# Value projection by halves of the contraction, the scaling of two attention heads on VectorE, and other PSUM banks at two places of the FFN

## What is computed

```python
D_MODEL, SEQ, DEPTH, D_FF = 1024, 256, 2, 2816       # D_A = D_B = 384, D_C = 256, B_HEADS = 6
...
def swiglu(x, w_gate, w_up, w_down):
    return (jax.nn.silu(x @ w_gate) * (x @ w_up)) @ w_down
...
def forgetting_attention(q, k, v, log_f):
...
        logits = logits + (c[:, :, q0:q1, None] - c[:, :, None, :q1])
...
        p = jax.nn.softmax(logits, axis=-1)
        outs.append(jnp.einsum('bhqk,bhkd->bhqd', p, vb))
...
def hybrid_mixer(x, w_in, ...):
    z = x @ w_in
    cuts = [int(v) for v in np.cumsum([D_A, D_A, D_B, D_B, D_B, B_HEADS])]
    a_x, a_gate, q, k, v, f_logit, c_u = jnp.split(z, cuts, axis=-1)
...
    o = jnp.concatenate([rms_norm(out_a, g_a), rms_norm(out_b, g_b), rms_norm(out_c, g_c)], axis=-1)
    return o.astype(x.dtype) @ w_out
...
    for l in range(DEPTH):
        x = layer_norm(ALPHA * x + 0.5 * swiglu(x, ffn1...), ln1_g[l], ln1_b[l])
        x = layer_norm(ALPHA * x + hybrid_mixer(x, ...), ln2_g[l], ln2_b[l])
        x = layer_norm(ALPHA * x + 0.5 * swiglu(x, ffn2...), ln3_g[l], ln3_b[l])
```

## Time and profile before

| | us |
|---|---|
| median of 3 runs | 1021.7 |
| lowest, highest | 1020.07, 1022.95 |
| the profiled execution | 1024.93 |
| its span on the core | 1023.1 |
| granted TensorE clock, mean | 0.989 |
| TensorE busy | 983.3 |
| VectorE busy | 700.4 |
| ScalarE busy | 538.8 |
| GpSimd busy | 332.3 |

### The profile page before, as it was taken

One profiled execution on the slowest core, in us unless ns is written; L12 is line 12 of the kernel. 1 busy time (PEld: TensorE's weight loads), 2 busy tenths in 40 slices (PEclk: granted clock), 3 DMA queues, 4 the chain that ended last, 5 costly groups with the idle time before them and its releaser, 6 DMA issues.

```text
span 1023.1 us, 14125 instructions
## 1 busy us (share of the span) xinstructions
PE 983.3 (96%) x5702; PEld 858.1 (84%) x5702; DVE 700.4 (68%) x820; ACT 538.8 (53%) x682; POOL 332.3 (32%) x398
## 2 busy tenths in 40 slices
PE   7899999999899999999999999999998989999997
PEld 6788888889887888888888888888988888888885
DVE  5676755788787756565788775657896876656556
ACT  4454545548883444444546444563788545444551
POOL 3029993042540600000053599900714342000000
PEclk9999999999999999999999999999999999999999
DMA  9755554474144665656476565545622356555541
GB/s 301 223 177 194 189 181 165 128 203 154 53 129 160 206 198 174 205 170 200 140 221 235 176 200 171 187 156 180 178 84 83 125 192 220 174 197 186 185 165 41
DMA packets 142383, 176.52 MB, mean 173 GB/s; under 512 B 11312, under 2 KB 126704, under 8 KB 142320
## 3 DMA queue, kind: packets, MB, share of 16 engines
q1 hardware_dynamic: 140592, 169.35, 51.8%
q0 software_dynamic: 1728, 6.29, 1.8%
HBM read 174.56 MB, written 1.05 MB: 172 GB/s over the span
## 4 chain that ended last, share of the span: by engine, by line
PE 82%; DVE 8%; ACT 3%; issue 2%; SPq 2%; POOL 2%; DMA 1%; DVEq 0%; POOLq 0%
PE bank L1691 28%; PE bank L1693 14%; PE bank L1662 11%; PE bank L1664 11%; PE bank L1663 11%; PE bank L1667 2%; SPq L430 2%; DVE wlo L1120 1%; ACT whi L714 1%; DMA raw<-in_ffn_w_up 1%; ACT u L922 1%; PE bank L1815 1%; POOL lngb L666 1%; PE bank L2005 1%; DVE xT_f L1377 1%
## 5 line engine op out<-in xcount | busy, mean ns | idle before, releaser
L1120 DVE TENSOR_TENSOR wlo<-raw,whi 128x2048 fp32r<-128x2048 f32 (+1 forms) x157 | 390.4, 2495 | 117.6 <-ACT whi L714 116.8
L1691 PE MATMUL bank<-xT,whi 128*128 128x512 f32 x1280 | 456.0, 400 | 6.2 <-DVE uT L1144 3.5
L1693 PE MATMUL bank<-xT,wlo 128*128 128x256 f32 x1280 | 360.0, 281 | 0.0
L714 ACT ACTIVATE whi<-raw 128x2048 fp32r<-128x2048 f32 (+1 forms) x157 | 297.2, 1897 | 14.8 <-DMA raw<-in_ffn_w_up 6.1
L1691 PEld LDWEIGHTS bank<-xT,whi 128*128 128x128 f32 x1280 | 241.2, 188 | 67.2 <-DVE uT L1144 4.9
L1693 PEld LDWEIGHTS bank<-xT,wlo 128*128 128x128 f32 x1280 | 242.5, 189 | 1.2
L1662 PE MATMUL bank<-whi,act_hi 128*128 128x512 f32 x376 | 148.7, 395 | 0.0
L1664 PE MATMUL bank<-whi,act_lo 128*128 128x512 f32 x376 | 146.9, 391 | 0.0
L1663 PE MATMUL bank<-wlo,act_hi 128*128 128x512 f32 x376 | 146.7, 390 | 0.0
L545 POOL TENSOR_TENSOR xtok<-xn,lngb 128x1024 f32<-128x1024 f32 x10 | 30.2, 3018 | 332.2 <-DVE xT L1409 332.2
L762 ACT ACTIVATE gs<-bank 128x512 f32<-128x512 f32 x40 | 23.9, 598 | 170.4 <-PE bank L1693 170.4
(11 more groups left out here) (318 smaller groups left out, 1337.7 us busy)
## 6 DMA issues: line engine op xcount, KB each, us to landing
raw<-in_ffn_w_up SPq DMA_DIRECT2D x44, 1024.0 KB, 5.4
raw<-in_ffn_w_down SPq DMA_DIRECT2D x44, 1024.0 KB, 4.9
raw<-in_ffn_w_gate SPq DMA_DIRECT2D x43, 1024.0 KB, 5.3
raw<-in_w_in SPq DMA_DIRECT2D x12, 1024.0 KB, 5.3
raw<-in_w_out SPq DMA_DIRECT2D x8, 1024.0 KB, 5.1
raw<-in_w_in SPq DMA_DIRECT2D x12, 512.0 KB, 5.1
lngb<-in_ln_g POOLq DMA_DIRECT2D x6, 512.0 KB, 4.1
lngb<-in_ln_b POOLq DMA_DIRECT2D x6, 512.0 KB, 5.5
```

Source lines behind the costliest of these rows:

```text
L714: A.activation(piece(whi, n, 8, PC)[:, :, cols], piece(raw, n, 8, PC)[:, :, cols], ACT.Copy).then_inc(hi_done, 1)
L1120: V.tensor_tensor(piece(wlo, n, 8, PC)[:, :, cols], piece(raw, n, 8, PC)[:, :, cols], piece(whi, n, 8, PC)[:, :, cols].bitcast(F32), ALU.s ...
L1691: T.matmul(bank[bnk + ft][:, :], hi[:, k, c], xT[:, k, :, :].rearrange("p a n -> p (a n)"), start=k == 0, stop=False)
L1693: ins = T.matmul(bank[bnk + ft][:, 0:SEQ], lo[:, k, c], xT_hi[:, k, :], start=False, stop=k == KD - 1)
```

## The change

1. **Value projection.** Pieces 0 and 1 of the mixer now hold the same 390 columns for contraction tiles 0 to 3 and 4 to 7. Events 0 and 2 sum in one bank (0), events 1 and 3 in another (1). There are 48 matmuls of 390 columns in a layer and not 48 of 256 and 48 of 134. Both splits have 1560 columns and not 2048 and 1072, and each load 1560 columns. The copies out are two for each token tile; the semaphore `f_evac` is gone, and the counts in `z_free` follow.
2. **Scaling.** Heads 0 and 1 are scaled on VectorE, between its reciprocals and the splits of pieces 8 and 9 (`ahead_mix(6)` and `ahead_mix(7)`). Heads 2 to 5 stay on GpSimd.
3. **FFN entry.** The up rows of token tile 1 go to bank 6 and not 5. TensorE waits for the Silu of tile 0 ahead of them, and no longer for the product ahead of the second half of `gate(f, 1)`.
4. **Parameters.** The wait for `par_ready` moves from ahead of `gate(f, 2)` to between its halves.

```diff
@@ -78,11 +78,11 @@
 QCOL = 2 * DA
-ZPIECES = [4 * DA, 4 * DA + PC, NIN - DC, 0, PC, None, None, None, 2 * PC]
+VCOL, VW = 4 * DA, DB + HEADS
+ZPIECES = [None, None, NIN - DC, 0, PC, None, None, None, 2 * PC]
...
-VT_W = DB - PC + HEADS
...
+        def body(t, n):
+            width = 4 * VW if n % LAYER_N in (MIX_BASE, MIX_BASE + 1) else 8 * PC
+            return t[:, slot(n), 0:width]
...
-        TOK_BANKS = ((6, 7), (4, 5))
+        TOK_BANKS = ((6, 7), (4, 6))
 
         def z_bank(e):
-            return (0, 2, 1, 3)[e] if e < 4 else 5 if e < 6 else e % 2
+            return e % 2 if e < 4 else 5 if e < 6 else e % 2
...
@@ block.sync @@
                 for m, col in enumerate(ZPIECES):
-                    if col is None:
+                    if m < 2:
+                        load(mix + m, win[L, :, 4 * m:4 * m + 4, VCOL:VCOL + VW], 4, VW)
+                    elif col is None:
...
@@ block.gpsimd @@
                 pool.wait_ge(ys_gelu, 16 * L + 16)
-                attn_scale(0)
-                attn_scale(1)
                 pool.wait_ge(oc_done, 2 * L + 2)
...
@@ block.scalar @@
-                A.activation(piece(whi, n, 8, PC)[:, :, cols], piece(raw, n, 8, PC)[:, :, cols], ACT.Copy).then_inc(hi_done, 1)
+                A.activation(body(whi, n), body(raw, n), ACT.Copy).then_inc(hi_done, 1)
...
-                    if f == 0:
-                        split_hi(base + FFN_N + 1, slice(0, VT_W))
-                    else:
-                        ahead(base + LAYER_N + 1)
+                    ahead(base + FFN_BASE[f] + FFN_N + 1)
...
                 def values_out(t):
-                    z_wait(t)
-                    A.activation(vv[:, t, 0:PC], bank[2 * t][:, 0:PC], ACT.Copy).then_inc(ly.z_evac, 1)
                     z_wait(2 + t)
-                    A.activation(flog[:, t, :], bank[2 * t + 1][:, DB - PC:VT_W], ACT.Copy).then_inc(f_evac, 1)
-                    A.activation(vv[:, t, PC:], bank[2 * t + 1][:, 0:DB - PC], ACT.Copy).then_inc(ly.z_evac, 1)
+                    A.activation(flog[:, t, :], bank[z_bank(t)][:, DB:VW], ACT.Copy).then_inc(ly.z_evac, 1)
+                    A.activation(vv[:, t, :], bank[z_bank(t)][:, 0:DB], ACT.Copy).then_inc(ly.z_evac, 1)
...
@@ block.vector @@
-                V.tensor_tensor(piece(wlo, n, 8, PC)[:, :, cols], piece(raw, n, 8, PC)[:, :, cols],
-                                piece(whi, n, 8, PC)[:, :, cols].bitcast(F32), ALU.subtract).then_inc(lo_done, 1)
+                V.tensor_tensor(body(wlo, n), body(raw, n), body(whi, n).bitcast(F32), ALU.subtract).then_inc(lo_done, 1)
...
                     if n == 0:
-                        split_lo(base + FFN_N + 1, slice(0, VT_W))
+                        split_lo(base + FFN_N + 1)
...
-                    vec.wait_ge(f_evac, 2 * L + 2)
+                    vec.wait_ge(ly.z_evac, 3)
...
+                def attn_scale(h):
+                    vec.wait_ge(ly.rrec_done, h + 1)
+                    V.tensor_scalar(prob[h % 2][:, 0:P], prob[h % 2][:, 0:P], rrec[:, h, 0:1], None, ALU.mult)\
+                        .then_inc(ly.pn_done, 1)
+                    V.tensor_scalar(prob[h % 2][:, P:], prob[h % 2][:, P:], rrec[:, h, 1:2], None, ALU.mult)\
+                        .then_inc(ly.pn_done, 1)
...
                 blocks_out()
                 attn_recip(0)
+                attn_scale(0)
                 attn_recip(1)
+                attn_scale(1)
                 ahead_mix(6)
...
@@ block.tensor, first_pair @@
+                    pe.wait_ge(ly.silu_done, f * (PAIRS + 1) + 1)
                     rows(u, 1, TOK_BANKS[1][1]).then_inc(pieces_used, 1)
...
@@ block.tensor, gate @@
                     if q == 1:
                         pe.wait_ge(ly.silu_done, silu_count(f, 0))
-                        features(base + gate_pos(f, q), 4, (ly.hid_done, silu_count(f, 0)))
+                        features(base + gate_pos(f, q), 4)
                     else:
                         pe.wait_ge(parts_added, gate_sums_done(L, f, q - 1))
-                        features(base + gate_pos(f, q), 4)
+                        features(base + gate_pos(f, q), 4, (par_ready, L + 1) if f == 0 and q == 2 else None)
...
                     down(f, 0)
-                    if f == 0:
-                        pe.wait_ge(par_ready, L + 1)
                     gate(f, 2)
...
@@ block.tensor, z_free and z_event @@
-                        pe.wait_ge(ly.z_evac, {6: 1, 7: 2}.get(e, e - 3))
+                        pe.wait_ge(ly.z_evac, {6: 2, 7: 4}.get(e, e - 3))
...
+                    c = slice(h * P, (h + 1) * P)
+                    if e in V_EVENTS:
+                        hi, lo = piece(whi, n0, 4, VW), piece(wlo, n0, 4, VW)
+                        k0 = 4 * (e // 2)
+                        for k in part:
+                            ins = mm3(bank[z_bank(e)][:, 0:VW], xT_hi[:, k0 + k, c], xT_lo[:, k0 + k, c], hi[:, k, :],
+                                      lo[:, k, :], k0 + k == 0, k0 + k == KD - 1)
+                        if part[-1] == 3:
+                            ins.then_inc(ly.z_half if h == 0 else pieces_used, 1)
+                        return
...
-                z_event(0)
-                z_event(2, range(0, KD // 2))
+                z_event(0, range(4))
+                z_event(2, range(0, 2))
                 turn_rows(ly, 0, 1)
-                z_event(2, range(KD // 2, KD))
+                z_event(2, range(2, 4))
                 pe.wait_ge(ly.xT_lo_done, 4)
-                z_event(1)
-                z_event(3)
+                z_event(1, range(4))
+                z_event(3, range(4))
```

More of the change, by code:

```diff
@@ L299, in trunk @@
         q_ones = sem("q_ones")
-        f_evac = sem("f_evac")
         oc_done = sem("oc_done")
@@ L709, in _, with split_hi @@
             A = nc.scalar
-            def split_hi(n, cols=slice(None)):
+            def split_hi(n):
                 act.wait_ge(raw_loaded[slot(n)], loaded(n))
-                A.activation(piece(whi, n, 8, PC)[:, :, cols], piece(raw, n, 8, PC)[:, :, cols], ACT.Copy).then_inc(hi_done, 1)
+                A.activation(body(whi, n), body(raw, n), ACT.Copy).then_inc(hi_done, 1)
             act.wait_ge(const_pool, 11)
@@ L1116, in _, with split_lo @@
                             ALU.subtract).then_inc(lo_done, 1)
-            def split_lo(n, cols=slice(None)):
+            def split_lo(n):
                 vec.wait_ge(hi_done, n + 1)
-                V.tensor_tensor(piece(wlo, n, 8, PC)[:, :, cols], piece(raw, n, 8, PC)[:, :, cols],
-                                piece(whi, n, 8, PC)[:, :, cols].bitcast(F32), ALU.subtract).then_inc(lo_done, 1)
+                V.tensor_tensor(body(wlo, n), body(raw, n), body(whi, n).bitcast(F32), ALU.subtract).then_inc(lo_done, 1)
             for L in range(DEPTH):
@@ L1901, in z_event @@
                     z_free(e)
+                    c = slice(h * P, (h + 1) * P)
[8 more added lines that the diff above has]
+                        return
                     hi, lo = piece(whi, n0, 8, PC), piece(wlo, n0, 8, PC)
-                    c = slice(h * P, (h + 1) * P)
                     for k in part:
-                        if e in V_EVENTS:
-                            n = PC if e < 2 else VT_W
-                            ins = mm3(bank[z_bank(e)][:, 0:n], xT_hi[:, k, c], xT_lo[:, k, c], hi[:, k, 0:n],
-                                      lo[:, k, 0:n], k == 0, k == KD - 1)
-                        else:
-                            ins = mm3(bank[z_bank(e)][:, z_cols(e)], hi[:, k, c], lo[:, k, c], xT_hi[:, k, :],
-                                      xT_lo[:, k, :], k == 0, k == KD - 1)
+                        ins = mm3(bank[z_bank(e)][:, z_cols(e)], hi[:, k, c], lo[:, k, c], xT_hi[:, k, :],
+                                  xT_lo[:, k, :], k == 0, k == KD - 1)
                     if part[-1] == KD - 1:
```

## The result

| | before | after |
|---|---|---|
| median | 1022.3 (4 runs) | 1012.15 (4 runs) |
| lowest, highest | 1020.07, 1024.04 | 1011.38, 1013.22 |
| profiled execution | 1024.93 | 1013.22 |
| its span, mean granted clock | 1023.1, 0.989 | 1011.3, 0.983 |

A forecast was written before the change was run, and what follows sets the result against it. TensorE, busy 96% of the span, was taken to bound the kernel. Gains of 4.2 + 3.0 + 9.0 + 2.8 = 19.0 us took the profiled 1024.93 to 1005.9, with the median 3.2 lower: 1002.7 us, range 997 to 1010.

The forecast's parts named there:

- The sum of waits and work: All four terms without regained clock: 2.5 + 3.0 + 5.7 + 2.8 = 14.0 us saved.
- the 5.0 of clock: Half-clock stretches behind the parameter wait (1.7 us) and the scaling waits (3.3 us), expected to return to full clock.
- Term 1: Parameter wait in layer 0's gate: covered by the gate's first half, 2.5 us of wait plus 1.7 of clock, 4.2 us.
- Term 2: FFN entries: three waits for the gate and up product go, 3.5 - 0.6 + 0.1 = 3.0 us gained.
- the falls vanish: Rival: clock falls behind the two second-FFN entries vanish since everything before them moves, 999.3 us; chance 0.13.
- Term 3: First two heads scaled on VectorE: 6.0 us of waits, 3.3 of clock, 0.3 given back, 9.0 us gained.
- Term 4: V projection: 48 matmuls of 390 columns, next event 1.4 us earlier per layer, 2.8 us gained.
- The wait of 1.96 grows to some 2.2: V projection: TensorE's wait ahead of token tile 1 grows because the transposes start 0.6 us earlier.
- a fall in both layers: Sign of being wrong: the clock falls behind the V projection in both layers.
- the later wait of `s5_outputs` is unchanged: Within the V projection term: VectorE's chain to the S5 outputs starts from block copies that wait for that same projection.
- the first rival: Waits go but their clock doesn't come back, or ScalarE gives the time back: gain 14.0, 1007.7 us; chance 0.17.
- the fall in the V projection: Rival: the longer wait there lets the clock fall in both layers, 2 x 1.7 us, 1006.1 us; chance 0.15.

The follow-up runs named there:

- the filled kernels: The changed kernel and the kernel before, each with useless matmuls put into TensorE's long waits: 1001.4 and 1015.15 us.
- experiment 1: The changed kernel with nine useless matmuls of 256 columns in the wait ahead of the S5 outputs, both layers: 1006.3 us.
- Experiment 5: The changed kernel with the old value projection, other three edits kept, run twice: 1008.3 and 1007.5 us; the changed kernel, timed again beside the second: 1012.1.

## Why the prediction was wrong, step by step

**The sum of waits and work was right.** 14.0 us forecast (the 19.0 without the 5.0 of clock), 13.2 measured at full clock, 13.7 between the filled kernels.

**Term 1, parameters: 4.2 forecast, 4.1 found.** (4.81 less the 0.70 of the entry, in the table of starts.) VectorE's copy now runs at 42.81, beside the first half of the gate, and TensorE does not stop. I had it stay where it was; it came 0.83 us earlier, about as much as TensorE, which did no harm; the clock is 1.00 where the earlier trace rows had 0.64.

```profile
42.81 0.26 DVE L1259 COPY par<-bank 128x104 f32<-128x104 f32 x1
...
42.76 0.40 PE L1698 MATMUL bank<-xT,whi 128*128 128x512 f32 x1
```

**Term 2, FFN entries: 3.0 forecast, 3.7 found without the clock.** The waits of the earlier trace rows are gone; `act_lo`, for which I took 0.6 off, shows 0.2 in all. The starts move by 0.7 us at the first entry and by 3.2 at each second FFN's entry, 1.7 of it because the fall of the clock there did not recur in this execution (rival "the falls vanish"), so 0.7 + 1.5 + 1.5 are the waits. In the profile of experiment 1 the falls are back.

**Term 3, scaling: 9.0 forecast.** Between the gates and the third head's scores the starts gain 5.0 and 4.8 us in this profile, 9.8 in all; alone and over several executions it is about 7. The work is as sized: 0.47 us from one head to the next on VectorE against 0.45 assumed. Compare, where one such instruction took 4.46 us on GpSimd:

```profile
263.64 0.29 DVE L1582 TENSOR_SCALAR lngb<-lngb,rrec 128x128 f32<-128x128 f32 x1
263.84 0.35 DVE L1584 TENSOR_SCALAR lngb<-lngb,rrec 128x256 f32<-128x256 f32 x1
264.11 0.16 DVE L1578 RECIPROCAL rrec<-rsum 128x2 f32<-128x2 f32 x1
```

**Term 4, V projection: 2.8 forecast; here the forecast failed.** The work is as sized (the loads are 780 KB each on the page and not 799, which changes nothing). The distance between starts at 390 columns is (207.12 - 204.09) / 17 = 0.178 us; where the clock stayed up (after, second profile) the stage took 216.56 - 203.92 = 12.64 us against 14.07 before, 1.4 a layer, with the new wait for `wlo` at 0.24 where 0.4 was forecast:

```profile
203.92 0.34 PE L1669 MATMUL bank<-whi,xT 128*128 128x390 f32 x1
...
216.56 0.39 PE L1669 MATMUL bank<-xT,whi 128*128 128x256 f32 x1 [0.24 <-DVE wlo L1119]
```

What failed is what the term takes the clock to do, in two places. "The wait of 1.96 grows to some 2.2": it did, to 2.18, and the term has no fall behind it; I gave that 0.15 as a rival, and named a fall in both layers as a sign of being wrong. It fell in both layers of the first profile:

```profile
211.94 0.44 PE L1669 MATMUL bank<-whi,xT 128*128 128x390 f32 x1 [2.18 <-DVE xT L1407]
212.22 0.41 PE L1670 MATMUL bank<-wlo,xT 128*128 128x390 f32 x1
212.43 0.53 PE L1671 MATMUL bank<-whi,xT 128*128 128x390 f32 x1
212.75 0.53 PE L1669 MATMUL bank<-whi,xT 128*128 128x390 f32 x1
```

(0.32 us apart from 212.43 on.) That the wait grew need not be the reason: over all profiles the clock fell behind 8 of 12 waits of 2.18 us, but also behind 3 of 8 of the old 1.96 us (both layers with the scaling alone), though behind neither in before. And "the later wait of `s5_outputs` is unchanged": it is not. It was 1.36 us, and is 1.09 in the first profile and 1.27 in the second; above all its place is another. A wait of 1.1 us with small matmuls behind it can cost 4.7 to 4.9 us: the clock was not full again before the dense matmuls of the next projection event. No case of mine had a stretch that costs more than 1.7 us. With the new value projection half clock costs 14.5 us and with the old one 8.1 (4.0 to 15.2), so this term was 2.6 - 6.4, a loss of nearly 4 us where a gain of 2.8 was forecast.

**The clock as a whole.** I counted falls to be regained (5.0 us) and none to be gained, since the earlier trace rows show full clock "wherever no long idle preceded". That was one execution. The cost of half clock in before varies from 8.1 to 14.3 us over 44 executions; the change moves everything and so draws again. In the two profiles all five short falls of before are gone (8.5 us), those that I counted on among them, and three short falls and two long stretches have come (15.3 us). So the first rival, that the clock behind the old waits does not come back (1007.7), is not what happened; the second, the fall in the V projection (1006.1), did happen in that profile, with the fall at 516 us and the long stretches on top, which no rival had. With the measured cost put in, the forecast reads 19.0 - 5.0 (nothing regained on balance) - 3.8 (lost) = 10.2 us, against 13.2 - 3.8 = 9.4 by the means and 9.0 by the medians of the two.

**What stays open.** Why the value projection alone saves 4.4 us at full clock and only 2.6 to 2.9 beside the other edits; the roughness of the split, some 2 us, may be all of it. And why the S5 outputs start at a bad place against the beat so often with the new value projection. In the profiles of after (two) and of after with the V wait filled (one) the clock fell behind the wait in both layers, six times in six, with the value projection alone in one layer of two; with all but the value projection in both layers of one execution and in neither of the other, and in before and with the scaling alone never. Experiment 5 shows which place is bad, not what puts the kernel there.

## What to carry to other kernels

Read a TensorE wait with what stands behind it: ahead of dense matmuls 1.8 to 2.2 us cost at most 1.7 us more, ahead of small ones 1.1 us could cost 5. One profile without a fall does not say that the wait is harmless: the same wait of the same kernel goes either way from one execution to the next. Split each execution into span times mean clock and the rest before you judge an edit; a gain of 2.6 us of work was hidden by 6.4 of clock. A few matmuls that nobody needs, in a bank that is free and with operands that are there already, are cheaper than a fall; half of the wait was enough here. Before real work is moved into a wait, look up every semaphore that it waits for.

## What the runs showed of the hardware

- The clock fell or did not fall behind the same wait of the same kernel: 1.37 us ahead of the S5 outputs, 2.18 us in the value projection (fell at 212.4 in one execution of after, not in the other).
- Every change of the clock in one execution lies a whole number of equal steps behind the first full clock, in all 16 profiles; that first point came between 10.52 and 17.48 us. Waits of 1.07 to 1.37 us ahead of the S5 outputs brought a long stretch 9 times in 9 when the next step came 1.3 to 2.7 us after their end, and never in the other 5 cases.
- At half clock the S5 tiles take 1.28 us and not 0.67, and the clock came back 10.2 us later, near the next dense matmuls. With dense matmuls behind the wait a fall cost some 1.7 us each time.
- From 256 over 390 to 512 columns the time of a matmul at full clock grows evenly with its columns: 0.119, 0.178, 0.231 us from start to start. 134 columns take 0.108, nearly as much as 256.
